# One of the 4 MB weight loads of turn 9 cut into a 24 KB-per-partition load and sixteen eight-partition loads

## What is computed

```
def expert_block(args):
    xblk, e = args
    act = swiglu_clamped(xblk @ w_gate_up[e] + b_gate_up[e])
    return act @ w_down[e] + b_down[e]
```

## Time and profile before

| | |
|---|---|
| median of 3 runs | 1217.13 us (1215.69 to 1217.30) |
| the profiled execution, its own time | 1217.35 us |
| its span | 1215.5 us |
| mean granted TensorE clock | 0.981 |
| TensorE matmul busy | 1138.6 us, 94% of the span |
| moved by DMA | 457.21 MB, mean 376 GB/s |

### The profile page before, as it was taken

One profiled execution on the slowest core, in us unless ns is written; L12 is line 12 of the kernel. 1 busy time (PEld: TensorE's weight loads), 2 busy tenths in 40 slices (PEclk: granted clock), 3 DMA queues, 4 the chain that ended last, 5 costly groups with the idle time before them and its releaser, 6 DMA issues.

```text
span 1215.5 us, 12312 instructions
## 1 busy us (share of the span) xinstructions
PE 1138.6 (94%) x5359; PEld 579.1 (48%) x5360; DVE 392.5 (32%) x619; ACT 202.3 (17%) x273; POOL 8.4 (1%) x19
## 2 busy tenths in 40 slices
PE   7999999999999999989898989999999859999887
PEld 6788888873344343424242424343443224443336
DVE  6964665641231221213030403131312111311226
ACT  5454545430010000101010101010100000000115
POOL 0000010000000000000000000000000000000000
PEclk9999999999999999999999998999999989999999
DMA  9855346898999999999999999999999999999990
GB/s 346 309 183 164 114 159 226 336 424 370 426 418 429 428 432 432 430 431 431 431 432 431 432 426 431 431 432 431 431 430 430 430 430 388 431 431 429 424 395 35
DMA packets 46700, 457.21 MB, mean 376 GB/s; under 512 B 4266, under 2 KB 5714, under 8 KB 29170
## 3 DMA queue, kind: packets, MB, share of 16 engines
q1 hardware_dynamic: 44832, 453.26, 89.5%
q10 hardware_dynamic: 1810, 3.12, 0.8%
HBM read 455.32 MB, written 1.05 MB: 375 GB/s over the span
## 4 chain that ended last, share of the span: by engine, by line
PE 67%; DMA 28%; DVE 3%; issue 1%; ACT 0%; DVEq 0%; ACTq 0%; POOLq 0%; POOL 0%
PE ps L690 65%; DMA ring<-in_up 17%; DMA ring<-in_down 11%; PE ps L996 1%; DVE w_split L1489 1%; PE ps L697 1%; DMA const<-in_const 0%; PE ps L1012 0%; DVE over_xn L1497 0%; DVE ring L1781 0%; DVE ring L1544 0%; DVE B L1731 0%; DVE B L1727 0%; DVE B L1728 0%; DVE w_split L1504 0%
## 5 line engine op out<-in xcount | busy, mean ns | idle before, releaser
L690 PE MATMUL ps<-ring,B 128*64 128x512 f32 (+1 forms) x2976 | 653.8, 594 | 42.3 <-DMA ring<-in_up 31.4
L690 PEld LDWEIGHTS ps<-ring,B 128*64 128x64 f32 (+1 forms) x2976 | 218.2, 139 | 463.4 <-issue 426.2
L1727 DVE TENSOR_SCALAR B<-ps 128x1024 f32<-128x1024 f32 x16 | 19.6, 1225 | 454.2 <-PE ps L996 372.8
L690 PE MATMUL ps<-w_split,over_BhT 128*128 128x512 f32 x480 | 151.9, 392 | 1.6 <-DVE ring L1548 1.5
L1489 DVE TENSOR_TENSOR w_split<-ring,w_split 128x1024 fp32r<-128x1024 f32 x87 | 104.7, 1223 | 67.8 <-ACT w_split L1234 67.3
L1234 ACT CAST w_split<-ring 128x1024 fp32r<-128x1024 f32 x87 | 90.4, 1053 | 101.6 <-PE ps L690 99.4
L690 PE MATMUL ps<-w_split,over_xn 128*128 128x512 f32 x256 | 99.7, 389 | 0.0
L690 PEld LDWEIGHTS ps<-w_split,over_BhT 128*128 128x128 f32 x480 | 89.7, 188 | 20.5 <-DVE ring L1548 1.9
L1358 ACT COPY B<-ps 128x512 f32<-128x512 f32 x28 | 15.0, 589 | 503.7 <-PE ps L996 503.7
L690 PE MATMUL ps<-const,xn 128*128 128x128 f32 x512 | 62.6, 282 | 9.6 <-DVE const L1696 9.1
L690 PEld LDWEIGHTS ps<-const,xn 128*128 128x128 f32 x512 | 60.9, 198 | 12.4 <-issue 12.4
(11 more groups left out here) (166 smaller groups left out, 491.7 us busy)
## 6 DMA issues: line engine op xcount, KB each, us to landing
ring<-in_up SPq DMA_DIRECT2D x47, 4096.0 KB, 31.0
ring<-in_down SPq DMA_DIRECT2D x22, 4096.0 KB, 29.0
ring<-in_up SPq DMA_DIRECT2D x26, 2048.0 KB, 18.5
ring<-in_down SPq DMA_DIRECT2D x16, 2048.0 KB, 21.6
ring<-in_w_in SPq DMA_DIRECT2D x28, 1024.0 KB, 6.2
ring<-in_up SPq DMA_DIRECT2D x14, 1024.0 KB, 10.1
ring<-in_w_branch SPq DMA_DIRECT2D x8, 1024.0 KB, 6.9
ring<-in_down SPq DMA_DIRECT2D x8, 1024.0 KB, 23.2
```

The costliest lines, as they stand in the source:

```text
L690: return pe.matmul(out, lhsT, rhs, start=start, stop=stop, skip_group_check=True)
L1727: step(ve.tensor_scalar(gate, two_banks(0), LIMIT, None, ALU.min))
```

## The change

In turn 9 the first 4 MB load (chunk g = `8 * PER_TURN` = 96, `in_up` of pair 9) is no longer one load. `load_by_low_engines` issues one load of the first 24 KB of each of the 128 partitions, and then sixteen loads for the last 8 KB: the p-th covers the eight partitions p, p + 16, ..., p + 112, 64 KB in all. All seventeen add 16 to the same semaphore, and `Ring` counts the place as having had 17 loads instead of 1. Nothing else is changed; the bytes, their places and the matmuls are the same.

```
+LOW_ENGINES, LOW_COLUMNS = 8, SLOT
+SHARED = (8 * PER_TURN,)
...
-            had[taken[0]] += 1
+            had[taken[0]] += 1 + (P // LOW_ENGINES if g in SHARED else 0)
...
+            def load_by_low_engines(to, w, signal):
+
+                columns = 2 * UNITS * SLOT - LOW_COLUMNS
+                sp.dma_start(to[:, 0:columns], w[:, 0:columns]).then_inc(signal, 16)
+                apart = P // LOW_ENGINES
+                for p in range(apart):
+                    sp.dma_start(to[p::apart, columns:], w[p::apart, columns:]).then_inc(signal, 16)
...
-                w = t["down" if down else "up"][pair, q // 2]
-                sp.dma_start(to, w.rearrange("p j h n -> p (j h n)")).then_inc(loaded[at], 16)
+                w = t["down" if down else "up"][pair, q // 2].rearrange("p j h n -> p (j h n)")
+                if g in SHARED:
+                    load_by_low_engines(to, w, loaded[at])
+                else:
+                    sp.dma_start(to, w).then_inc(loaded[at], 16)
```

## The result

The changed kernel takes 1225.16 us (median of six runs, 1224.77 to 1225.88) against 1217.22 us of the kernel before on the same chip; the ratio is 1.0065, with a 95% interval of 1.0055 to 1.0075, so +7.9 us. The forecast was 1223.4, slower, with a range of 1216.3 to 1227.6.

A forecast was written before the change was run, and what follows sets the result against it. The 16 DMA engines bound the stream, TensorE waiting for the late half. Collision +10.7 us, less the 5 us lead, plus 0.6, gives 6.3 us: 1217.1 + 6.3 = 1223.4 us, range 1216.3 to 1227.6.

The forecast's parts named there:

- The path: After turn 9, whatever the change does to the landing at about 977.6 us reaches the end one for one.
- The collision: In the small loads, engines writing where others stream slow each other; chance 0.58 with the early half, range 1221 to 1227.
- The factor: Slowdown of the small loads' packets, 1.8 x 1.5 = 2.7: sixteen packets take 13.1 us, less 2.4, so +10.7 us.
- The lead of the eight engines: The small loads' engines stand in the early half, 5 us ahead; 0.6 us was added for one a little nearer.
- The 8.7 busy engines of the windows at 1010 us: Mean DMA share 0.54 as queues run dry, read as about half the engines running about 5 us behind.
- 6.3: Forecast delay in us of the landing at 977.6, and so of the end.
- the GB/s of the slice: In the changed load's slice GB/s was to fall little.
- No effect: Rival: nothing collides, or the rows don't stay on the same eight engines; 1216 to 1217.5 us, chance 0.23.
- faster: Rival: no collision and all eight engines fully 5 us ahead, landing at 977.6 2.4 us sooner; 1214.7 us, chance 0.07.
- The wrong eight: Rival: the eight engines are the late half; 1219.6 us without collision, 1228 to 1229 with; chance 0.07.
- SP never got stuck: Rival: a full queue blocks SP's small issues, delaying the next load to 752 or so; 1219 to 1223 us, chance 0.05.
- The run-dry windows at the end: Around 1010 us engines run dry one by one; forecast to last longer after the change, over 10 us.

The follow-up runs named there:

- Experiment 12: The changed kernel with the split made to the first 4 MB load of turn 4 instead of turn 9: 1225.06 us, ratio 1.0065 to the kernel before.
- experiment 3: The changed kernel with each small load's eight partitions 4 apart inside blocks of 32, not 16 apart: 1223.72 us, ratio 1.0061 to the kernel before.
- experiment 5: The changed kernel with eight small loads, 4 apart, for partitions 0 to 63 only, the others' last 8 KB unloaded: 1215.90 us, ratio 0.9992 to before.
- 7: The changed kernel with eight single-partition small loads, all in one engine's own partitions, other last 8 KB unloaded: 1214.44 us, ratio 0.9979 to before.
- 9: The changed kernel with eight small loads of four partitions, four engines writing into others' partitions, other last 8 KB unloaded: 1219.50 us, ratio 1.0017 to before.
- experiment 10: The changed kernel with small loads, 4 apart, for partitions 64 to 127 only, the others' last 8 KB unloaded: 1221.40 us, ratio 1.0030 to before.
- 1: The changed kernel with the last 8 KB of all 128 partitions as one load instead of sixteen: 1216.2 us, ratio 1.0001 to the kernel before.
- 2: The changed kernel with the last 8 KB in eight loads of sixteen partitions, 8 apart: 1222.91 us, ratio 1.0046 to the kernel before.
- experiment 4: The changed kernel with the same destinations but eight neighbouring source rows in each small load: 1225.88 us, ratio 1.0074 to the kernel before.
- 8: The changed kernel with sixteen small loads of eight neighbouring partitions each, instead of 16 apart: 1224.60 us, ratio 1.0066 to the kernel before.

## Why the prediction was right, and where it was not

**The path** held. The landing at 977.6 moved by 8.1 us, and the end by 7.9. Experiment 12 shows the same from 290 us further away.

**The collision** held, as a kind. Experiments 3, 5 and 7 against the change, 9 and 10 show that it is a matter of whose rows and partitions an engine handles; 1 and 2 leave nothing for the pieces or the shares, and 4 nothing for the distance between the rows read. That the writing is what collides, and not the reading, rests on experiment 4 beside 8, where the same reads gave packets of two lengths; it is likely, not proven. The Trainium skill's rule on ports ("SBUF — State Buffer", "Door 1: The DMA port swizzle") says which partitions belong together: experiment 3 changed speed at partition 64, where by that rule the low engines leave their own ports, and not within 0 to 63.

**The factor** was mis-sized. I reckoned 2.7 for engines that meet three at a time, 13.1 us for the sixteen packets; they take 0.57 us each, factor 1.9, so 9.2 us: 3.9 us less. No run shows a third engine making it worse: with eight engines at partitions 64 to 127 only, 4 apart, where each meets one streaming engine, the packets take 0.63 us (experiment 10), in the change 0.57. How often three did meet in the change no trace tells, since the engines are microseconds apart.

**The lead of the eight engines** is the step that failed. "They stand in the early half, 5 us ahead" took 5 us off (and put 0.6 back). Experiment 3 shows six of them within 2.0 us of the first and two 3.2 and 3.9 us behind it, that is among the late ones; experiment 5 the same with nothing slowed. What the latest of the eight lose counts in full. The 8.7 busy engines of the windows at 1010 us could not tell who was who.

**What I had not in the sum:** that engines outside the collision are slow too. The two late engines were slowed already in their 24 KB packets (1.6 instead of 0.91 us for the 3 to 4 us before they got to the small ones), about 1.5 us. With this the sum for them is 9.2 - 2.4 + 1.5 = 8.3 us, measured 8.2 at the next landing. So 6.3 was two errors of opposite sign, -3.9 and +4.4, and one omission, +1.5; that the forecast came within 1.8 us of the measurement is in good part luck. The same omission made one of its signs wrong: the GB/s of the slice was to fall little, since only the colliding engines were thought slow, and it fell from 431 to 338.

**The rivals.** No effect and faster are out. The wrong eight was partly true: two of eight. SP never got stuck, at 0.563 us an issue. The run-dry windows at the end look as they should if the engines are now spread otherwise, no longer in two halves: from 1018 to 1023 us the share falls steadily,

```profile
1018.00:1019.00 1.00, 1.00 (x8) 0.38 (x6) 0.00 (x0) 0.00 (x0) 0.00 (x0) 1.00 0.76 328
...
1020.00:1021.00 1.00, 1.00 (x8) 0.33 (x6) 0.00 (x0) 0.00 (x0) 0.00 (x0) 1.00 0.38 164
...
1022.00:1023.00 1.00, 1.00 (x6) 0.29 (x4) 0.00 (x0) 0.00 (x0) 0.00 (x0) 1.00 0.15 66
```

where before it stood near a half for five microseconds. In single packets: before, six engines end that load from 1010.6 to 1011.2, one at 1013.0 and nine from 1015.0 to 1017.1; now three end it from 1014.3 to 1014.7, two at 1017.5 and 1017.8 and eleven from 1019.2 to 1022.0. The clear division into early and late engines is gone, but they are not nearer together: 7.7 us from the first to the last, against 6.5 (over 10 was forecast). Whatever there was of evening out, it was paid for with more than it could ever give: 2.4 us at best, against the 6.6 us that the stream lost.

## What to carry to other kernels

In this stream of loads, which never pauses, what the engines that are behind lost came out at the end, wherever it was lost (experiment 12); so a gain from evening out 16 DMA engines must be weighed against what the evening-out does to the stream. A transfer over part of the partitions isn't a smaller transfer: ask which engine carries each row, and whether that engine, or another, is at home there. Before moving work to "the early engines", find out from single packets which ones they are.

## What was not expected of the hardware

One engine writing into another's partitions slowed just two, to half (0.61 us for 8 KB, 2.2 to 2.4 us for 32 KB). Four such engines slow the whole stream: 247 GB/s of 431, and slow packets on engines that meet nobody; eight give 246, and eight loading eight neighbouring partitions at a time, though microseconds apart, 265 to 305. Where between one and four it tips, and what it is that all engines share, stays open; no run had two or three. An issue for eight rows on SP takes 0.563 us, that of a 4 MB load of 128 rows 0.328, and those of the 1 MB loads of line 661 0.43.
